# Weights behind the gathered rows are requested when row 252 has landed instead of row 254

## The reference

```python
u = expert_down[eidx]
a = jax.nn.gelu(jnp.einsum('thkd,td->thk', u, xb), approximate=False)
coef = (g * a.astype(jnp.float32)).astype(xb.dtype)
return jnp.einsum('thk,thkd->td', coef, expert_up[eidx])
...
return rmsnorm(h, g_final)          # end of the first block
...
h = rms_norm(x, norm_mix[i])        # start of the second block
u = h @ w_in[i]
```

## Time and profile before

| | |
|---|---|
| median of 3 runs | 1385.02 us (1383.69 to 1385.59) |
| the profiled execution | 1384.36 us, of which the span of the profile is 1382.6 us |
| TensorE busy | 1250.5 us, 90% |
| VectorE busy | 949.9 us, 69% |
| ScalarE busy | 587.7 us, 43% |
| GpSimd busy | 273.1 us, 20% |
| row gathers (queue q0) | 268.45 MB |
| weights and other transfers of SyncE (queue q1) | 126.10 MB |

### The profile page before, as it was taken

One profiled execution on the slowest core, in us unless ns is written; L12 is line 12 of the kernel. 1 busy time (PEld: TensorE's weight loads), 2 busy tenths in 40 slices (PEclk: granted clock), 3 DMA queues, 4 the chain that ended last, 5 costly groups with the idle time before them and its releaser, 6 DMA issues.

```text
span 1382.6 us, 15300 instructions
## 1 busy us (share of the span) xinstructions
PE 1250.5 (90%) x5488; PEld 860.0 (62%) x5488; DVE 949.9 (69%) x1976; ACT 587.7 (43%) x1047; POOL 273.1 (20%) x281
## 2 busy tenths in 40 slices
PE   9999998988787878878787778899999999999998
PEld 8887897533343433434243224488788888888887
DVE  5767667977867677777776776755756556777445
ACT  5657553323223232322323233465556744654334
POOL 1000002443444344343433334100000000000000
PEclk9999999999999999999999999999999999999999
DMA  7543437999999999999999999745355445555551
GB/s 290 206 167 121 169 128 291 421 421 421 421 420 422 421 421 420 421 415 420 406 424 421 421 413 409 307 159 179 122 187 177 153 155 183 179 183 184 197 197 61
DMA packets 57266, 398.71 MB, mean 288 GB/s; under 512 B 7128, under 2 KB 7640, under 8 KB 9448
## 3 DMA queue, kind: packets, MB, share of 16 engines
q0 software_dynamic: 36864, 268.45, 46.8%
q1 hardware_dynamic: 18288, 126.10, 25.5%
q10 hardware_dynamic: 2040, 3.19, 0.7%
HBM read 396.67 MB, written 1.05 MB: 288 GB/s over the span
## 4 chain that ended last, share of the span: by engine, by line
PE 59%; DMA 30%; DVE 6%; ACT 3%; issue 1%; POOL 0%; SPq 0%; ACTq 0%; DVEq 0%; POOLq 0%
PE ps L854 36%; DMA B<-in_ex,eidx 29%; PE ps L1238 10%; PE ps L882 4%; DVE B L2588 3%; PE ps L883 2%; ACT diags L1799 1%; ACT hl L1523 1%; DVE hl L2102 1%; DMA ring<-in_wt 1%; PE ps L1117 1%; PE ps L1099 1%; ACT av_ L1792 0%; PE ps L958 0%; POOL B L818 0%
## 5 line engine op out<-in xcount | busy, mean ns | idle before, releaser
L1238 PE MATMUL ps<-B,diags 128*128 128x512 f32 x1024 | 480.8, 614 | 114.2 <-ACT diags L1799 114.0
L1238 PEld LDWEIGHTS ps<-B,diags 128*128 128x128 f32 x1024 | 187.6, 193 | 378.6 <-issue 190.4
L2588 DVE CUSTOM_DVE_ANT_0 B<-B 128x1024 f32<-128x1024 f32 x256 | 311.4, 1221 | 119.0 <-DMA B<-in_ex,eidx 118.9
L818 POOL DMA_INDIRECT B<-in_ex,eidx x256 | 267.0, 1043 | 595.2 <-PE ps L1238 363.7
L2102 DVE TENSOR_TENSOR hl<-ring,hl 128x2048 fp32r<-128x2048 f32 x110 | 251.6, 2290 | 168.9 <-ACT hl L1523 168.7
L1523 ACT ACTIVATE hl<-ring 128x2048 fp32r<-128x2048 f32 x110 | 210.1, 1912 | 128.2 <-PE ps L854 125.3
L854 PE MATMUL ps<-hl,R 128*128 128x512 f32 x912 | 212.0, 391 | 0.3 <-DVE R L2118 0.3
L854 PE MATMUL ps<-hl,XT 128*128 128x512 f32 (+1 forms) x888 | 205.5, 390 | 3.0 <-DVE hl L2102 2.5
L1792 ACT ACTIVATE av_<-av_ 128x2 f32<-128x2 f32 x128 | 26.0, 203 | 421.8 <-DVE av_ L2588 421.8
L854 PEld LDWEIGHTS ps<-hl,R 128*128 128x128 f32 x912 | 169.9, 188 | 36.0 <-DVE R L2118 0.7
L854 PEld LDWEIGHTS ps<-hl,XT 128*128 128x128 f32 x888 | 163.6, 189 | 39.0 <-DVE hl L2102 4.0
(11 more groups left out here) (377 smaller groups left out, 1022.2 us busy)
## 6 DMA issues: line engine op xcount, KB each, us to landing
ring<-in_wt SPq DMA_DIRECT2D x112, 1024.0 KB, 4.8
raw<-in_wt SPq DMA_DIRECT2D x4, 1024.0 KB, 8.5
B<-in_ex,eidx POOLq DMA_INDIRECT x256, 13.7
X<-in_x SPq DMA_DIRECT2D x2, 512.0 KB, 4.6
B<-in_mem ACTq DMA_DIRECT2D x1, 1024.0 KB, 8.2
PW<-in_wple SPq DMA_DIRECT2D x1, 1024.0 KB, 7.1
ring<-in_wt SPq DMA_DIRECT2D x2, 512.0 KB, 4.1
out<-B SPq DMA_DIRECT2D x3, 256.0 KB, 2.0
```

The lines of the kernel that those rows point to most:

```text
L818: e.indirect_dma_start(out=rows[i % NG][:, :], out_offset=None, in_=A["ex"], in_offset=bass.IndirectOffsetOnAxis(ap=eidx[:, tb, s:s + 1], ...
L1238: m = e.matmul(acc[tb][hf][:, :], diags[:, i % 4, :], rows[i % NG][:, 1024 + 512 * hf:1536 + 512 * hf], start=(s == 0), stop=(s == 127))
L2588: m = e.tensor_tensor_reduce(R[:, 0:1024], R[:, 0:1024], XG[:, tb, :], 1.0, 0.0, ALU.mult, ALU.add, av_[:, tb, s + z:s + z + 1])
```

## The change

SyncE's wait ahead of GV is for row 252 instead of row 254. Nothing else is altered.

```diff
                 if n == GV:
-                    e.wait_ge(*gath[254])
+                    e.wait_ge(*gath[252])
                     e.dma_start(loaded(n)[:, 0:1024], A["wt"][FIRST[name] + 2 * k + h][:, 0:1024]).then_inc(gv_first[0], 16)
                     e.dma_start(loaded(n)[:, 1024:2048], A["wt"][FIRST[name] + 2 * k + h][:, 1024:2048]).then_inc(ld[n][0], 16)
                     continue
```

## The result

The changed kernel takes 1386.99 us, the median of 11 runs (1383.49 to 1390.26). The kernel before, run beside it, takes 1383.69 us (11 runs, 1381.86 to 1385.59). The ratio is 1.0020, with a 95% interval from 1.0012 to 1.0028: the change costs 2.8 us by the ratio, between 1.7 and 3.9, and 3.3 us by the two medians. The forecast was 3.4 us and a median of 1388.4, in a range from 1384.4 to 1390.6. The profiled execution has a span of 1384.1 us, 1.5 us more than before.

What follows compares the result with a forecast made beforehand. The prediction took row 255's landing, set by one late DMA engine, to bound the kernel at this place. Gain 0, row delay 2.0 and clock 1.4 us sum to 3.4 us, giving a median of 1388.4 (range 1384.4 to 1390.6).

Steps and rivals of the forecast that it cites:

- What bounds the kernel: At the last rows, nothing can start before row 255 lands, and one late DMA engine alone sets when.
- The gain of 0: Weights requested 5.9 us earlier gain 0, as both halves already land 0.7 to 1.1 us before their use.
- The delay of 2.0 us: On the late engine, row packets taking turns with weight packets make row 255 land 2.0 us later.
- number of turns: Of 20 row packets left on the late engine, 7 go ahead and 13 take turns with 4 KB weight packets.
- The two ends of the bounds: Row 255's delay on the late engine: 0 if all row packets go first, 3.7 us if turns start at once.
- turns from the first packet: Rival: on the late engine weights and rows alternate at once, 3.7 us plus 1.4 for the clock, 1390.1; chance 0.09.
- rows first: Rival: the late engine serves all 20 row packets before weights, delay 0, 1385.0 us; chance 0.16.
- The clock's 1.4 us: TensorE, idle 2.1 us ahead of the last eight matmuls, runs them at the lower clock; 1.4 us, bounds 0 and 1.6.
- a low clock under the last eight matmuls is somewhat likelier than not: 5 of 12 similar TensorE idle times were followed by the lower clock; the idle time might grow to 3.2 us.
- The rival's price for the twelve matmuls: Rival, faster: the twelve matmuls at 892.65 miss the low clock, worth 1.3 us, and another block too; 1382.4, chance 0.04.
- The sum: Whole kernel: 0 gain, 2.0 us for the late row and 1.4 us for the clock make 3.4 us slower.

Runs made afterwards that it cites:

- row255: The kernel before with the wait ahead of the weight requests set to row 255 instead of row 254; ratio 1.0002 to the kernel before.
- the filled pair: Kernel before and changed kernel, each with unread matmuls added in TensorE's idle times around the last rows; medians 1383.42 and 1385.71 us, ratios 1.0001 and 1.0015.
- next_first: The changed kernel with the whole half behind GV (8 KB packets) requested ahead of GV's two pieces; ratio 1.0025 to the kernel before.
- row250: The changed kernel with the wait set to row 250 instead of 252; ratio 1.0060 to the kernel before (4 runs).
- only_gv: The changed kernel with only GV's two pieces requested at row 252, the halves behind it at row 254; ratio 1.0023 to the kernel before.
- quarters: The changed kernel with GV requested in four pieces of 512 columns (2 KB packets) instead of two; ratio 1.0019 to the kernel before.
- row253: The changed kernel with the wait set to row 253 instead of 252; ratio 1.0007 to the kernel before.

## Why the prediction was right, and where it was off

**What bounds the kernel.** Right. Row 255's landing releases the chain in the changed kernel too: its dot product is released by the landing after 2.53 us of idle time, and from its start to the last eight matmuls it takes 2.15 us, as before.

**The gain of 0.** Right. In the changed kernel the half behind GV lands at 873.91 + 12.5 = 886.4 and is used at 889.07; before it landed at 886.7 for a use at 887.41. More time to spare, and no one who waited for it. row255 shows the other side: weights become the bound only when they are requested some 2 us later still.

**The delay of 2.0 us.** Right in place and size: 1.97 us more between the dot products of rows 253 and 255, and a landing after 16.5 us (16.6 was forecast). The forecast's number of turns also gave 3.3 (measured 3.28) for larger packets, 1.0 (1.12) for smaller, 6.5 (6.3) for row 250 and 0.6 to 0.8 (0.64) for row 253. The two ends of the bounds are refuted: turns from the first packet would have cost 3.7 us at row 252, and rows first nothing.

The number of turns was right, but partly by luck, for both numbers that it is the difference of were too small. The forecast had 20 row packets left when the weights arrive, 7 of them ahead, and 13 in turn. In the kernel before, the time from 874.2 to the last row packet at 881.2 is 7.0 us, or 22 to 23 packets of 0.31 us: row 253 landed 3.4 us after row 252, and not the 2.47 us on which the 20 rest. And more than 7 went ahead. The first weight packet on an idle engine moves 0.96 us after the request in the kernel before. The turns begin 4.4 us after the request in the change, so 3.5 us, the time of about 11 packets, passed on the late engine between. 11 were then left, with two short ones of 4 bytes, and the 12 weight packets came among them. The experiments test the one-for-one turns and the length of a packet; the 7 they don't test, since all of them were worked out with it.

The rule of the Trainium skill, "DMA: Bandwidth & Descriptors", section "Queues, rings and completion order", is that an engine goes round its queues packet by packet. The trace agrees from 877.49 us on, where every row packet but one has a gap for one weight packet ahead of it. For the 4.4 us up to there it does not, and the delay of 1.97 us instead of 3.7 decides against turns from the first packet.

**The clock's 1.4 us.** Wrong in size. The step "a low clock under the last eight matmuls is somewhat likelier than not" didn't hold in two profiles of the change: the block took 3.70 us both times, behind idle times of 1.52 and 1.50 us. The idle time was shorter than the 2.1 forecast because the eight matmuls ahead of it ended later than was counted. The forecast had allowed for their lower clock and put their end at 883.7, 6.9 us after row 253's dot product; in the changed kernel they end at 884.0, 7.5 us after it. The sum at L2520 starts 5.89 us after row 255's dot product, against 6.08 before, so the clock took nothing from this execution. Against the filled pair it took 0.5 us (medians) to 1.0 us (ratios) on average, which can't be told from 0. With longer delays, next_first and row250, the low clock did come under the last block, at idle times of 4.52 and 4.10 us; in next_first the sum starts 7.59 us after the dot product.

**The rival's price for the twelve matmuls.** Wrong. I had priced the low clock under the twelve matmuls at 892.65 at 1.3 us. They ran at full clock in the changed kernel (3.02 us, against 4.61 in the earlier trace rows), and it bought nothing. TensorE's next block is in the timeline of the kernel before and of the changed one:

```profile
898.49 8.46 PE L854 MATMUL ps<-hl,XT 128*128 128x512 f32 x36 [0.36 <-DVE hl L2102]
```

```profile
899.98 0.50 PE L854 MATMUL ps<-hl,XT 128*128 128x512 f32 x1 [1.96 <-DVE hl L2102]
```

Both wait for VectorE's remainder, 0.36 us in the one and 1.96 us in the other. From the sum at L2520 to this block it is 10.7 us in both. So the low clock at this place is hidden by VectorE in the kernel before, which is a reason why filling could not make it faster. It is not hidden everywhere: in row255, where the twelve started later and took 5.49 us, the next block starts 11.4 us behind the sum.

**The sum.** 3.4 us were forecast, 2.8 measured (1.7 to 3.9; 3.3 by the medians), 2.9 when measured again (1.7 to 4.2). The profiles show 2.0 us of it at row 255 and none from the clock; what makes up the rest is not shown, and it may be noise. The median came out 1.4 us lower than forecast, and 1.3 of this is that the kernel before was that much faster in the runs beside it than in the three that the forecast starts from. Against 0.2% the result is on the edge: 0.50 for slower and 0.46 for within was a fair account of it.

## What to carry to other kernels

A transfer that starts on idle DMA engines isn't free if one engine still carries what the compute waits for: the last landing, not the mean share, is the critical path. Look for a DMA share of one sixteenth ahead of a wait. In this kernel each packet of a newcomer that got a turn there cost its own length, so smaller packets cost less, and so did a request that left fewer turns. And asking for data earlier is worth something only where an engine waits for its landing today.

## What was not expected of the hardware

A newcomer on a DMA engine that is busy with another queue waits long for its first turn, and from then on the two alternate packet by packet. From the request to the first turn on the late engine it was 4.43 and 4.44 us in the change's two profiles, 4.43 in only_gv, 4.46 in next_first, 4.15 in quarters, and 3.47 in row253. Less the 0.96 us that a first packet takes on an idle engine, this is the time of 8 (row253) to 11 row packets. What sets it, a count of packets, their bytes or a time, is not shown, since all row packets have 8 KB. Packets of 4 bytes, which end a transfer, take a turn as well.

An added matmul of 128 float32 columns took 0.23 to 0.26 us, while a transpose through TensorE of the same width took 0.13 (eight in 1.04 us).
